# Even and odd columns for the two products of a weight slab in a feed-forward layer

## What is computed

```
D_MODEL, SEQ, DEPTH, D_FF = 1024, 256, 2, 2816

def swiglu(x, w_in, w_out):
    a, b = jnp.split(x @ w_in, 2, axis=-1)
    return (jax.nn.silu(a) * b) @ w_out

x = x + 0.5 * swiglu(rmsnorm(x, ffn1_norm[l]), w_ffn1_in[l], w_ffn1_out[l])
...
x = x + 0.5 * swiglu(rmsnorm(x, ffn2_norm[l]), w_ffn2_in[l], w_ffn2_out[l])
```

## Time and profile before

| | us |
|---|---|
| median of three runs (2860.0 to 2866.12) | 2864.21 |
| the profiled execution: its span, which is all that the profile gives of its own time | 2861.2 |
| PE busy | 2805.8 (98%) |
| PE loading weights | 2669.5 (93%) |
| DVE busy | 1842.9 (64%) |
| ACT busy | 1299.2 (45%) |
| mean granted clock of TensorE | 0.996 of full speed |

### The profile page before, as it was taken

The page is one execution under the profiler, slowest core; times in us unless marked ns, Lnnn a source line. Parts: engine busy times, 40 slices in busy tenths (PEclk is TensorE's granted clock), DMA queues, the critical chain, the costliest instruction groups (busy, mean ns, idle before and its releaser), DMA issues.

```text
span 2861.2 us, 51128 instructions
## 1 busy us (share of the span) xinstructions
PE 2805.8 (98%) x21992; PEld 2669.5 (93%) x21992; DVE 1842.9 (64%) x3008; ACT 1299.2 (45%) x1860; POOL 71.9 (3%) x66
## 2 busy tenths in 40 slices
PE   8999999999999999999999999999999999999998
PEld 8999799999999889999999888799999998888998
DVE  5668576665666766766666557666666654666665
ACT  5445444444444545444444334444464433544443
POOL 0000000000000010000000001100000000110000
PEclk9999999999999999999999999999999999999999
DMA  7554366555555445555565653355555566435553
GB/s 257 180 166 130 111 173 203 177 183 186 189 168 169 112 149 177 176 179 179 192 208 160 187 145 116 96 178 191 177 175 180 168 195 141 133 89 166 180 184 108
DMA packets 481282, 474.52 MB, mean 166 GB/s; under 512 B 47105, under 2 KB 464417, under 8 KB 480929
## 3 DMA queue, kind: packets, MB, share of 16 engines
q1 hardware_dynamic: 477472, 460.75, 51.5%
q0 software_dynamic: 3584, 10.49, 1.4%
HBM read 464.91 MB, written 6.29 MB: 165 GB/s over the span
## 4 chain that ended last, share of the span: by engine, by line
PE 90%; DVE 5%; ACT 3%; DMA 1%; issue 1%; SPq 0%; DVEq 0%; ACTq 0%
PE ps L945 33%; PE ps L1044 33%; PE ps L1065 16%; PE ps L1182 2%; PE ps L1106 2%; DVE WL L1875 1%; PE ps L1151 1%; ACT WH L1496 1%; PE ps L992 1%; PE ps L996 1%; PE ps L988 1%; DMA RAW<-in_w_in 0%; PE ps L976 0%; DMA RAW<-in_w_branch 0%; DVE REGION L2030 0%
## 5 line engine op out<-in xcount | busy, mean ns | idle before, releaser
L1875 DVE TENSOR_TENSOR WL<-RAW,WH 128x2048 fp32r<-128x2048 f32 (+2 forms) x390 | 871.5, 2240 | 414.6 <-ACT WH L1496 412.6
L1496 ACT ACTIVATE WH<-RAW 128x2048 fp32r<-128x2048 f32 (+2 forms) x398 | 736.8, 1864 | 162.3 <-DMA RAW<-in_w_in 83.9
L1065 PE MATMUL ps<-HL,WH 128*128 128x256 f32 x1408 | 394.0, 280 | 0.0
L1065 PE MATMUL ps<-HH,WH 128*128 128x256 f32 x1408 | 393.6, 280 | 0.0
L1065 PE MATMUL ps<-HH,WL 128*128 128x256 f32 x1408 | 393.0, 279 | 0.0
L945 PE MATMUL ps<-UH,WH 128*128 128x256 f32 x1328 | 382.6, 288 | 3.4 <-DVE WL L1875 3.4
L1044 PE MATMUL ps<-UH,WH 128*128 128x256 f32 x2688 | 374.8, 282 | 0.5 <-DVE WL L1875 0.5
L945 PE MATMUL ps<-UL,WH 128*128 128x256 f32 x1328 | 374.5, 282 | 0.0
L945 PE MATMUL ps<-UH,WL 128*128 128x256 f32 x1328 | 374.3, 282 | 0.0
L1044 PE MATMUL ps<-UL,WH 128*128 128x256 f32 x2688 | 373.4, 281 | 0.0
L1044 PE MATMUL ps<-UH,WL 128*128 128x256 f32 x2688 | 373.3, 281 | 0.0
(11 more groups left out here) (326 smaller groups left out, 3710.0 us busy)
## 6 DMA issues: line engine op xcount, KB each, us to landing
RAW<-in_w_ffn_in SPq DMA_DIRECT2D x88, 1024.0 KB, 5.1
RAW<-in_ffn_wi SPq DMA_DIRECT2D x88, 1024.0 KB, 5.1
RAW<-in_w_in SPq DMA_DIRECT2D x86, 1024.0 KB, 5.5
RAW<-in_w_ffn_out SPq DMA_DIRECT2D x32, 1024.0 KB, 4.9
RAW<-in_ffn_wo SPq DMA_DIRECT2D x32, 1024.0 KB, 5.0
RAW<-in_w_out SPq DMA_DIRECT2D x16, 1024.0 KB, 5.0
RAW<-in_w_ffn_out SPq DMA_DIRECT2D x16, 768.0 KB, 4.2
RAW<-in_ffn_wo SPq DMA_DIRECT2D x16, 768.0 KB, 4.2
```

What stands on the lines that cost most here:

```text
L1065: last = nc.tensor.matmul(bank(n + side, 0, T), a[:, k, side * P:(side + 1) * P], b[:, k0 + k, :], start=k0 + k == 0 and a is wh and b is ...
L1496: nc.scalar.activation(split_ap(s, part_high(s)), raw_ap(s), ACT.Copy).then_inc(weights_high, 1)
L1875: v_.tensor_tensor(split_ap(s, part_low(s)), raw_ap(s), split_ap(s, part_high(s)).bitcast(FP), ALU.subtract)\
```

## The change

A slab's product of side 0 now takes the even columns and side 1 the odd ones, so PE reads each row of weights with a step of two elements (8 bytes) where it read neighbours. The same 48 matmuls of a slab are issued in the same order. Hidden tile 2j + side now holds features 256j + 2p + side on partition p. So the rows of the second matrix are loaded in that order: even tiles of a slab by one DMA, odd tiles by a second, each with half of the rows, 1 KB a row as before. ACT's and DVE's splitting, line 1065 and all other matmuls are untouched; `opening` keeps the old columns for its other caller.

```
-                pl.slabs(name + ".out", [2 if t == len(PARTS) - 1 else 0], split=True, words=kt * 256, places=over)
+                pl.slabs(name + ".out", [2 if t == len(PARTS) - 1 else 0], dmas=2, split=True, words=kt * 256, places=over)
...
-                        load(s, (slot(s, kt, 256), rows(wo[k0 * P:(k0 + kt) * P, q * 256:(q + 1) * 256])))
+                        src = wo[k0 * P:(k0 + kt) * P, q * 256:(q + 1) * 256].rearrange("(j p two) n -> two p j n", p=P, two=2)
+                        load(s, *[(slot(s, kt, 256)[:, side::2, :], src[side]) for side in range(2)])
...
-            def opening(n, s, u):
+            def opening(n, s, u, every=1):
...
+                def cols(side):
+
+                    return slice(side, 256, 2) if every == 2 else slice(side * P, (side + 1) * P)
...
-                        nc.tensor.matmul(bank(n + side, 0, T), wh[:, k, side * P:(side + 1) * P], UH[:, k, :], start=k == 0, stop=False)
+                        nc.tensor.matmul(bank(n + side, 0, T), wh[:, k, cols(side)], UH[:, k, :], start=k == 0, stop=False)
...
-                        opening(p0, s, u)
+                        opening(p0, s, u, 2)
...
-                                last = nc.tensor.matmul(bank(n, 0, T), a[:, k, side * P:(side + 1) * P], b[:, k, :],
+                                last = nc.tensor.matmul(bank(n, 0, T), a[:, k, side:256:2], b[:, k, :],
                                                         start=i == 0 and k == 0, stop=i == 2 and k == DK - 1)
```

More of the change, by code:

```diff
@@ L991, in opening @@
                     for k in range(DK):
-                        nc.tensor.matmul(bank(n + side, 0, T), wl[:, k, side * P:(side + 1) * P], UH[:, k, :], start=False, stop=False)
+                        nc.tensor.matmul(bank(n + side, 0, T), wl[:, k, cols(side)], UH[:, k, :], start=False, stop=False)
                 for k in range(DK):
@@ L995, in opening @@
                     for side in range(2):
-                        last = nc.tensor.matmul(bank(n + side, 0, T), wh[:, k, side * P:(side + 1) * P], UL[:, k, :], start=False, stop=k == DK - 1)
+                        last = nc.tensor.matmul(bank(n + side, 0, T), wh[:, k, cols(side)], UL[:, k, :], start=False, stop=k == DK - 1)
                         if k == DK - 1:
```

## The result

The changed kernel takes 2870.69 us (median of five runs, 2869.04 to 2872.61), where the kernel before takes 2862.95 beside it (five runs, 2857.62 to 2866.12). The ratio is 1.0035, with a 95% interval of 1.0024 to 1.0045: a little slower, where 53.7 us less had been forecast. The profiled span grew by the same 7.7 us, from 2861.2 to 2868.9.

What follows compares the result with a forecast made beforehand. PE was taken as the bound, 98% busy. Gains of 4 x 7.0 + 3 x 7.3 + 2.0 + 7 x 0.26 = 53.7 us gave a 2807.5 us span, plus 3.0 for the median: 2810.5 us, range 2792 to 2868.

Steps and rivals of the forecast that it cites:

- What bounds the kernel: Whole kernel: PE is busy 98% of 2861.2 us, so only what shortens PE's work or makes it wait counts.
- That the distance depends on the addresses of the two reads: Line 1044: 119.8 ns a matmul in place 2 (bad), 116.9 in place 5 (better), by stream and weight addresses.
- The load still has 128 columns, but walks 1024 bytes instead of 512 in the same time: Line 1044's stepped load keeps pace with the stream, gaining 7.0 or 7.3 us a network, 2.0 in the fifth.
- The price of 111.5: Line 1044's assumed ns per matmul, from true float32 matmuls with equal load and stream speeds; bounds 108 and 116.9.
- That a load in pace with the stream meets it more cheaply: Line 1044: today's stream, twice as fast, passes the load once every matmul; at equal pace 111.5 ns was expected.
- slower: the stepped load: Rival for line 1044: a step of two halves fetch speed, adding 824 us; a milder form adds 50; chance 0.12.
- It decides from 118.5 ns a load on: Threshold in the slower rival: a stepped load sets PE's pace from 118.5 ns, a tenth above its columns' 108.
- Right: ... places 0 to 2 and 3 to 5 alike: Sign of success: line 1044 takes 112 to 113 us a network, with both groups of places alike.
- wrong: weight loads much longer than 190 ns: Sign of failure, the slower case: PE bound by weight loads much longer than 190 ns.
- DVE and ACT following, and the fifth network: Their loop takes 10.83 us a pair of slabs, charged nothing; DVE's 11.35 limits the fifth network's gain to 2.0 us.
- The transfers at nothing: Second matrix's split slab loads: landing 0.5 us later on each of 96 slabs, but costing PE nothing.
- Line 1065 is the same instructions on the same kind of data: nothing: Second matrix's matmuls: no gain or loss, still 117.8 ns each.

Runs made afterwards that it cites:

- run 1: Kernel before, but line 1044 streams one activation column 256 times, so the stream stands still beside the contiguous weight load: 2817.02 us.
- run 8: Kernel before with contiguous columns, a 224-byte gap ahead of place 0 and a 32-byte gap ahead of REGION: 2836.39 us, ratio 0.9917.
- run 7: Kernel before with contiguous columns and 32-byte gaps between the tiles of places 0 to 2, sweeping the weights' distance from the stream: 2850.8 us.
- run 3: Kernel before with only the two transfers per slab of the second matrix, rows in the old order: 2859.14 us, ratio 0.9995.
- run 4: Changed kernel with only the stepped columns, the second matrix loaded as before: 2872.08 us, ratio 1.0033.

## Why the prediction was wrong

**What bounds the kernel: right.** The loss is PE's distance from one matmul to the next, and the chain has it in line 1050.

**That the distance depends on the addresses of the two reads: right.** With the stream still, all places pay 111.67 ns (run 1), and with the same contiguous loads and other gaps the bad places lose their 120 (run 8): that is shown. That it is the distance between the two reads, and not the weights' own address beside a moving stream, rests on the second matrix and is likely, not shown. The rule of the Trainium skill that was weighed against it (SBUF — State Buffer, Who interferes with whom), PE's two read ports independent and PE never waiting, does not hold here as the prediction read it: 111.67 against 116.67 and 120.0 ns, with the same loads, is PE's stream costing PE's load. Why this is 8.3 ns at distance 0, 5.0 at 224 and other amounts in run 7 stays open, and so does whether it is the one read passing the other.

**"The load still has 128 columns, but walks 1024 bytes instead of 512 in the same time": this step failed.** It does not walk them in the same time. A matmul with it takes 117.8 ns beside a still stream and 120.0 beside a moving one, so the gain of 7 us a network became a loss of 1.3 to 1.6. The price of 111.5 came from a true float32 matmul, a row that has the right ratio of speeds but a contiguous load. Run 1 has nearly the same number, 111.67, for a contiguous load beside a still stream. Neither says anything of a stepped one. The prediction did write that no row shows a step, and then took its upper end from 116.9 "among the cases that gain", which kept the case that came out of the sum.

**That a load in pace with the stream meets it more cheaply: right in kind.** The stream's share fell from 5.0 and 8.3 ns to 2.2, alike at all places. That was worth 2.8 ns in the good places and 6.1 in the bad, and the step cost 6.1.

**The rival "slower: the stepped load": right in kind.** "It decides from 118.5 ns a load on": alone, at 117.8, the stepped load stays just below, and only with the stream's 2.2 does it come to 120.0, above. (120.0 - 118.5) x 8 x 1008 = 12 us is about the 11.6 that line 1050 lost. Its prices, half speed for 824 us or 5% above today's distance for 50, were too high. With the step a matmul is dearer by 5.5%, but 5.5% of 111.67 and not of today's 118.5. The rival had 0.12 and needed more, since nothing in the trace spoke against it. The sentence that spoke against it was the Trainium skill's (Advanced Engine Details and Errata, SBUF Cachelines): with two hits on a 16-byte line a read keeps full speed. The trace nearly agrees, two elements of each 16 bytes taking 117.8 ns where four take 111.67; with one element of each (a step of four) it is 233.2 ns, twice the 117.8. On a path that PE bounds, the 6.1 decide.

**"Right: ... places 0 to 2 and 3 to 5 alike" and "wrong: weight loads much longer than 190 ns":** the first sign was met, the second was not (196 ns), and the time was still longer. As tests they were too coarse: what told the cases apart was the level, 120.0 or 111.7, not that the places agree.

**DVE and ACT following, and the fifth network: right,** as run 1 showed, since the change itself never asked for it. At 111.67 ns the other networks keep one piece, the first loses 0.55 us, and the fifth is held at DVE's 11.33 us a pair, as the earlier trace rows had it. From its first to its last matmul line 1044 gained 1.2 us there, of the 2.0 in the sum, and 6.2 to 7.1 in the others.

**The transfers at nothing: right** (run 3). "Line 1065 is the same instructions on the same kind of data: nothing" was off by 2.9 us, in the other direction.

## What to carry to other kernels

An access pattern that no row shows has no price, however well the rest of the argument stands: run it alone, with its counterpart made still, before it is added to anything. When two reads get in each other's way by their addresses, move the addresses first; 256 bytes of gaps gained 0.83% here, the second matrix's share included, where changing the pattern lost 0.35%. A change that trades one cost for another should be measured as two, or its sum of nearly nothing hides both.

## What the runs showed that was not expected

Beside a still stream, a weight load of 128 columns holds PE to about 8.8 bytes a ns of the memory it walks (steps of two, three and four elements: 117.8, 173.3, 233.2 ns a matmul), above a floor of 111.67 ns that contiguous columns reach.

The second matrix, the same instructions on the same kind of data, takes 62.19 us in one network and 60.73 or 59.85 in another of the same program. At 62.19 it takes 117.8 ns a matmul in every place. At 60.73 its places differ, 116.6 ns in places 0 to 2 and 113.3 in 3 and 4, by their start times; at 59.85 all places take 113.3, and there run 8 has put all of them 192 bytes beyond a multiple of 256 from HH. So its addresses count too, but only in some networks. The changed kernel and run 4 have the 60.73 in the same two networks, though in run 4 only the first matrix's columns differ from the kernel before, which has it in none. What lets a network leave the 117.8 was not found.
